# Four whole-array products of the mixing stage: computed by GpSimd instead of VectorE

## The reference

```
r, k, v = token_shift_lerp(r_p, mu_r), token_shift_lerp(k_p, mu_k), token_shift_lerp(v_p, mu_v)
w = -softplus(-(w0 + tanh(xw) @ w2)) - 0.5;   decay = exp(-exp(w));   a = sigmoid(a0 + xa @ a2)
kk = normalised(k * k_k);   k = k * (1 + (a - 1) * k_a)
state_t = state_{t-1} * decay_t + (state_{t-1} a_t) b_t + v_t k_t,   y_t = state_t r_t     (a_t = -kk, b_t = kk * a)
bonus = sum(r * k * r_k, over a head) * v;   out = (groupnorm(y) + bonus) * g
```

## Time and profile before

| | us |
|---|---|
| median of 3 runs (1985.1 to 1989.57) | 1986.86 |
| the profiled execution | 1986.76 |
| its span, first to last instruction | 1985.0 |
| PE busy | 1939.5 (98%) |
| DVE busy | 1049.0 (53%) |
| ACT busy | 849.4 (43%) |
| POOL busy | 11.0 (1%), 23 instructions |

### The profile page before, as it was taken

One profiled execution on the slowest core, in us unless ns is written; L12 is line 12 of the kernel. 1 busy time (PEld: TensorE's weight loads), 2 busy tenths in 40 slices (PEclk: granted clock), 3 DMA queues, 4 the chain that ended last, 5 costly groups with the idle time before them and its releaser, 6 DMA issues.

```text
span 1985.0 us, 29402 instructions
## 1 busy us (share of the span) xinstructions
PE 1939.5 (98%) x11105; PEld 1646.5 (83%) x11105; DVE 1049.0 (53%) x1098; ACT 849.4 (43%) x964; POOL 11.0 (1%) x23
## 2 busy tenths in 40 slices
PE   8999999999999999999999799999999999999997
PEld 7888888888888889999999578888888888888886
DVE  5445444544444445788556735554444444544443
ACT  6444444444344446634432435544444444434443
POOL 1000000000000000000000000000000000000000
PEclk9999999999999999999999799999999999999998
DMA  7666666666666667554622246666666666666663
GB/s 237 191 191 190 190 190 190 190 182 189 190 191 192 190 197 235 154 150 126 185 85 78 99 126 183 211 191 190 189 187 186 190 190 190 190 187 196 191 193 125
DMA packets 194920, 353.60 MB, mean 178 GB/s; under 512 B 23760, under 2 KB 26064, under 8 KB 194576
## 3 DMA queue, kind: packets, MB, share of 16 engines
q1 hardware_dynamic: 194144, 352.23, 60.0%
q0 software_dynamic: 512, 0.06, 0.0%
q10 hardware_dynamic: 176, 0.07, 0.0%
HBM read 346.56 MB, written 5.77 MB: 177 GB/s over the span
## 4 chain that ended last, share of the span: by engine, by line
PE 93%; DVE 4%; DMA 1%; ACT 1%; issue 1%; SPq 0%; ACTq 0%; DVEq 0%
PE psA L314 39%; PE psB L314 38%; PE psB L730 5%; PE psA L730 4%; PE psT L555 1%; DVE wlo L299 1%; DMA raw<-in_w_in 1%; DMA x<-in_x 0%; DVE subst L922 0%; PE psM L1085 0%; DVE tinv L922 0%; PE psA L741 0%; PE psT L1067 0%; ACT whi L290 0%; DVE y L922 0%
## 5 line engine op out<-in xcount | busy, mean ns | idle before, releaser
L299 DVE TENSOR_TENSOR wlo<-raw,whi 128x1024 fp32r<-128x1024 f32 (+1 forms) x648 | 788.1, 1218 | 842.3 <-ACT whi L290 836.6
L290 ACT CAST whi<-raw 128x1024 fp32r<-128x1024 f32 (+1 forms) x648 | 676.6, 1046 | 955.9 <-PE psA L314 448.4
L314 PE MATMUL psA<-whi,xh 128*128 128x512 f32 (+1 forms) x736 | 283.9, 386 | 0.0
L314 PE MATMUL psA<-whi,xl 128*128 128x512 f32 (+1 forms) x736 | 283.4, 385 | 0.0
L314 PE MATMUL psA<-wlo,xh 128*128 128x512 f32 (+1 forms) x736 | 283.3, 385 | 0.0
L314 PE MATMUL psB<-whi,xh 128*128 128x512 f32 x704 | 275.9, 392 | 0.0
L314 PE MATMUL psB<-whi,xl 128*128 128x512 f32 x704 | 274.2, 389 | 0.0
L314 PE MATMUL psB<-wlo,xh 128*128 128x512 f32 x704 | 274.2, 389 | 0.0
L314 PEld LDWEIGHTS psA<-whi,xh 128*128 128x128 f32 x736 | 138.5, 188 | 27.4
L314 PEld LDWEIGHTS psA<-wlo,xh 128*128 128x128 f32 x736 | 138.5, 188 | 27.4
L314 PEld LDWEIGHTS psA<-whi,xl 128*128 128x128 f32 x736 | 138.4, 188 | 27.5
(11 more groups left out here) (373 smaller groups left out, 2190.4 us busy)
## 6 DMA issues: line engine op xcount, KB each, us to landing
raw<-in_ffn_w_gate SPq DMA_DIRECT2D x176, 512.0 KB, 3.7
raw<-in_ffn_w_up SPq DMA_DIRECT2D x176, 512.0 KB, 3.7
raw<-in_ffn_w_down SPq DMA_DIRECT2D x176, 512.0 KB, 3.7
raw<-in_w_in SPq DMA_DIRECT2D x80, 512.0 KB, 3.7
raw<-in_w_out SPq DMA_DIRECT2D x32, 512.0 KB, 3.7
x<-in_x SPq DMA_DIRECT2D x4, 512.0 KB, 7.4
x_dram<-x SPq DMA_DIRECT2D x4, 512.0 KB, 8.6
x<-x_dram SPq DMA_DIRECT2D x4, 512.0 KB, 6.7
```

The costliest lines, as they stand in the source:

```text
L290: nc.scalar.copy(whi[:, slot, :, 0:ncol], raw[:, slot, :, 0:ncol]).then_inc(hi_ready, 1)
L299: nc.vector.tensor_tensor(wlo[:, slot, :, 0:ncol], raw[:, slot, :, 0:ncol], whi[:, slot, :, 0:ncol].bitcast(F32), ALU.subtract).then_inc(l ...
L314: mm = nc.tensor.matmul(ps[:, tb, 0:ncol], lhs[:, k0 + t, tok], rhs[:, slot, t, 0:ncol], start=(first and t == 0 and p == 0), stop=(last a ...
```

## The change

The four products are issued by GpSimd, in one sequence ahead of and behind its clearing of `tt_all` and `tinv`. DVE no longer issues them; it waits for "kp" before `k_dec`, for "b_inv" before `b_dec`, for "r_dec" before `rk`, and for "bonus_v" before `y + bonus`. The lo parts of the groups keep their order and follow each other where the products stood.

```
         def mix_pool(pool):
+            need(pool, "kmul")
+            need(pool, "pinv")
+            pool.tensor_tensor(kmul[:, :, :], kmul[:, :, :], pinv[:, :, :], ALU.mult).then_inc(steps["kp"], 1)
+            pool.tensor_tensor(iclr[:, :, :], iclr[:, :, :], pinv[:, :, :], ALU.mult).then_inc(steps["b_inv"], 1)
             full(pool, "kn", 0)
             stored(pool, "kn", 0)
             pool.memset(tt_all[:, :, :], 0.0).then_inc(tt_zero, 1)
             pool.memset(tinv[:, :], 0.0).then_inc(t_zero, 1)
             pool.wait_ge(t_zero, 1)
             pool.memset(tinv[:, 0:1024:33], 1.0).then_inc(t_one, 1)
+            need(pool, "r1")
+            need(pool, "a_dec")
+            pool.tensor_tensor(chunks(r), chunks(r), chunks(pdec), ALU.mult).then_inc(steps["r_dec"], 1)
+            for i in range(2):
+                stored(pool, "bonus", i)
+            need(pool, "v1")
+            pool.tensor_tensor(bonus[:, :, :], bonus[:, :, :], v[:, :, :], ALU.mult).then_inc(steps["bonus_v"], 1)
...
             vdone(last, "kmul")
-            splits(24, 26)
-            need(V, "pinv")
-            vdone(tt(kmul[:, :, :], kmul[:, :, :], pinv[:, :, :], ALU.mult), "kp")
-            splits(26, 27)
+            splits(24, 27)
             in_out(2)
             lerp_chunk(2)
-            splits(27, 28)
-            vdone(tt(iclr[:, :, :], iclr[:, :, :], pinv[:, :, :], ALU.mult), "b_inv")
-            splits(28, 30)
+            splits(27, 30)
             vdone(V.tensor_copy(pend[:, :, :], chunks(pdec)[:, :, C - 1:C]), "pend")
             need(V, "kk_raw")
+            need(V, "kp")
             vdone(tt(k[:, :, :], k[:, :, :], kmul[:, :, :], ALU.mult), "k_dec")
...
+            need(V, "b_inv")
             vdone(V.scalar_tensor_tensor(iclr[:, :, :], iclr[:, :, :], -1.0, kk[:, :, :], ALU.mult, ALU.mult), "b_dec")
...
-            splits(44, 45)
-            vdone(tt(chunks(r), chunks(r), chunks(pdec), ALU.mult), "r_dec")
-            splits(45, 46)
+            splits(44, 46)
+            need(V, "r_dec")
...
-            splits(59, 61)
-            for i in range(2):
-                stored(V, "bonus", i)
-            vdone(tt(bonus[:, :, :], bonus[:, :, :], v[:, :, :], ALU.mult), "bonus_v")
-            splits(61, 67)
+            splits(59, 67)
...
+            need(V, "bonus_v")
             vdone(tt(y[:, half, :], y[:, half, :], bonus[:, half, :], ALU.add), f"y_bonus{i}")
```

More of the change, by code:

```diff
@@ L892, in build @@
             "max0", "max1", "exp0", "exp1", "prob0", "prob1",
-            "att_hi0", "att_hi1", "lora_wa", "lora_g", "tanh", "gsig", "k0", "k1", "v1", "kk_raw", "kk_sq", "kk_root", "kk_inv",
+            "att_hi0", "att_hi1", "lora_wa", "lora_g", "tanh", "gsig", "k0", "k1", "r1", "v1", "kmul", "kp", "b_inv", "kk_raw", "kk_sq", "kk_root", "kk_inv",
             "lsum", "p", "pinv", "rk", "a_dec", "b_dec", "r_dec", "k_dec", "bonus_v",
```

## The result

The changed kernel is slower: 1995.61 us (median of 6 runs, 1993.43 to 1996.0) against 1986.23 us for the kernel before (6 runs, 1983.17 to 1989.57). The ratio is 1.0045, 95% interval 1.0032 to 1.0058. The profiled execution took 1994.16 us, span 1992.4.

A forecast was written before the change was run, and what follows sets the result against it. PE, busy 98% of the span, was taken as the bound, with DVE mattering only where PE waits for it. Stalls of middle 5.65 us, 7.3 with the clock, on 1986.76 gave 1994; range 1985.7 to 1998.5.

The forecast's parts named there:

- No gain from the 9.1 us: Taking the four products off DVE gives PE 0, since none lies in 914.87 to 946.5, where PE waits for DVE.
- A product takes 4.5 us on GpSimd: Length of each of the four products on GpSimd: 4.5 us, range 3.6 to 5.4 us.
- the middle of two sums: Product length from the 1.80 us clearing: three arrays in turn 5.4 us, two inputs only 3.6 us; 4.5 us taken.
- A product holds DVE's two-input instructions for its length: While a GpSimd product runs, no DVE instruction with two SBUF inputs starts, and the other way round; chance 0.58.
- Both rivals without holding: No disturbance between the engines: 1987, chance 0.20. GpSimd yields, running only when DVE is idle: 1988.7, chance 0.14.
- the far longer product: Rival: a GpSimd product far longer than 5.4 us, with DVE held: above 1999, chance 0.05.
- kp and b_inv: 3.2 us if DVE keeps its turn, 4.3 if GpSimd takes it, and 1.65 for the clock: Groups 24 to 27: held lo parts make PE lose 3.2 or 4.3 us, plus 1.65 us once for a lower-clock group.
- the middle of both orders: Whole stalls, r_dec's 1.9 us included: 5.1 us if DVE keeps its turn, 6.2 if GpSimd takes it; middle 5.65.
- r_dec: 1.9 us: Behind groups 44 and 45, `rk` begins 2.3 us late; less 0.4 margin, PE loses 1.9 us at the "bonus" sums.
- DVE was to be first from a common signal: In a race from one signal DVE starts before GpSimd, so group 44's lo (881.88 to 883.1) goes ahead of r_dec.
- bonus_v: 0: After group 59's lo the product holds DVE until 951.0 or 952.1, before PE or ACT needs anything: 0 us.
- The total: Stalls of 5.65 us and 1.65 for the clock, 7.3 us over the profiled 1986.76: 1994.

The follow-up runs named there:

- number 7: The kernel before the change with the four products left out altogether, computed by no engine: ratio 0.9998 (0.9989 to 1.0008) to the kernel before.
- number 6: Changed kernel with b_inv delayed until group 32's lo is done, bonus_v until group 62's, r_dec back on VectorE: ratio 0.9999 to the kernel before.
- number 12: Changed kernel with kp and b_inv only multiplying their array by 1.0, without `pinv`; executed once, trace only: `kmul` to "kn" 26.83 us, 25.06 in the kernel before.
- number 4: Changed kernel with each GpSimd product replaced by clearings of the same array, about 4.5 us together: ratio 1.0001 (0.9992 to 1.0010) to the kernel before.
- numbers 1: Only kp and b_inv on GpSimd, r_dec and bonus_v on VectorE as before the change: ratio 1.0031 (1.0019 to 1.0044) to the kernel before.
- 2: Only r_dec on GpSimd, the other products on VectorE as before the change: ratio 1.0008 (0.9999 to 1.0017) to the kernel before.
- 3: Only bonus_v on GpSimd, the other products on VectorE as before the change: ratio 0.9999 (0.9990 to 1.0008) to the kernel before.
- 5: Changed kernel with each GpSimd product cut into eight products of 256 elements: ratio 1.0034 (1.0023 to 1.0046) to the kernel before.
- number 8: The kernel before with the lerp of v's first half moved ahead of group 52's lo on VectorE: ratio 1.0000 (0.9991 to 1.0009) to the kernel before.

## Why the prediction was right

- *No gain from the 9.1 us.* Shown by number 7 (0.9998), and by number 6 for three products done elsewhere.
- *A product takes 4.5 us on GpSimd.* Measured 4.62, 4.57 and 4.56 us without company. That the middle of two sums hit it is luck as far as the runs show: the sums had the time grow with the number of arrays moved at the clearing's rate, and in number 12, with one input less, GpSimd's rows were longer (5.7 and 6.4 us) and the holds shorter (3.4 us).
- *A product holds DVE's two-input instructions for its length.* Shown by groups 25 and 26 in the changed kernel, by number 4 for the reading as the cause, and by number 6 for the instruction that is not held. Both rivals without holding fall with these rows, and the far longer product with the 4.6 us.
- *kp and b_inv: 3.2 us if DVE keeps its turn, 4.3 if GpSimd takes it, and 1.65 for the clock.* GpSimd took it: the two alternate, one instruction each. PE waited 3.9 us in two pieces and is 5.9 us late at the sums behind. Three groups from 827.17 take 10.39 us where 2.88 each would be 8.64: 1.75 us for the clock, 0.91 in that stretch, so part of it at 1.2 GHz in place of 2.4. Behind the shorter waits of number 12 the clock stayed at full level (8.89 us for three groups). The 4.15 us besides the clock lie near the 4.3 of the order that came; the middle of both orders, 3.75, was 0.4 us low.
- *r_dec: 1.9 us.* Measured 1.8 in the trace, 0.08% alone (-0.01 to 0.17%). One detail was wrong: DVE was to be first from a common signal. At r1 GpSimd was first (887.74 against 887.84; alone too, both at 881.75) and group 44's lo waited out the whole product. The sum is the same since `rk` waits for both in either order, but PE's loss came as waits of 0.3 us at a group and 1.2 us at the sums, and some 0.2 us for starting again after each (a group takes 3.06 us behind a wait, 2.88 in a row).
- *bonus_v: 0.* Not quite in the trace: in the changed kernel group 59's lo was first, the product took the second turn, and PE then waited 0.65 us for group 60. Alone it measured 0.9999, without that wait. What the prediction had wrong is when PE needs group 60: it took that from the earlier trace rows, behind a group 59 of 4.53 us at the lower clock. Now group 59 takes 3.14 us, so PE comes 1.4 us sooner.
- *Why group 59 is shorter.* The stretch at the lower clock has moved to group 58, which takes 4.6 us (949.09 to 953.71) in place of 3.2. There it costs PE nothing, because the wait for group 59's lo takes it in: 0.81 us in place of 2.29. The traces of numbers 1 and 2 have it there too (waits of 1.84 and 0.80 us), those of 3, 5 and 7 have the 1.8 and 2.3 us of before. What decides where it falls is open. PE's 3.3 us of waits at groups 58 to 60 against 4.1 before are therefore no gain of the change.
- *The total.* Forecast 7.3 us over the profiled execution, 1994; the profiled pair differs by 7.4 us, the medians by 9.4. That 7.4 lies so near 7.3 is in part luck: 1.4 us are given back at groups 58 and 59, against 0.65 at group 60, 0.4 in the stalls and 0.3 between the "bonus" sums and group 59 that the sum didn't have. Such stretches come and go between executions of equal work: number 8, the same as the kernel before up to 911 us, has a granted clock of 1.00 in 830 to 880 where that one has 0.97. The part of 9.4 beyond 7.3 is not told apart from the spread of the runs (the kernel before: six from 1983.17 to 1989.57).

## What to carry to other kernels

Moving work to an idle engine pays only if the engine it leaves is what the bound one waits for, at that place: look where the chain runs through it, and which release starts that chain, before counting busy time. A GpSimd elementwise operation that reads SBUF isn't idle-engine work here: for its 4.5 us it held each VectorE instruction with two SBUF inputs that fell beside it in these traces, so it belongs where VectorE is idle, reads PSUM, or is several groups ahead. The 4 us that were to be had here lay in the order of VectorE's own instructions (the lo that PE waits for issued first, idle pieces filled), and took no second engine.

## What the runs showed of the hardware that was not expected

- A writing GpSimd isn't harmless to all of DVE: beside clearings a `TENSOR_SCALAR` of 128x4 from SBUF to SBUF took 0.87 us in place of 0.16 (number 4), ending at 817.49 with the clearing (817.47), and in number 12 0.76 us, to 821.38, with the end of GpSimd's row (821.36); two-input instructions beside the clearings kept their time.
- DVE and GpSimd alternated instruction by instruction where both had work queued; neither kept its turn (kp, group 25, b_inv, group 26).
- A GpSimd product of 256 elements takes 0.74 us, of 2048 elements 4.6: some 0.2 us per instruction and 2.15 ns per element, from these two.
- A multiplication by a constant on GpSimd (one input) had rows longer than a product of two arrays (5.7 to 6.4 us against 4.6 to 5.7; 5.2 us against 4.5 without the wait for a lo part) and let DVE go before they ended. This is one execution.
